# A hybrid two-layer trunk on one core: later constants, a mixing row in three transfers, and a shifted table of steps

## The reference, cut to what matters

```
h = rms_norm(x, norm_g[l]);  p = h @ w_in[l]                 # columns of p are split below
sb:  y_sb  = stick_breaking(sq, sk, sv) * silu(sg)           # 4 heads x 128
mla: q = rms_norm(rms_norm(c_q) @ mla_w_uq);  k, v from rms_norm(c_kv) @ mla_w_ukv and k_rope
     y_mla = block_causal_softmax(rope(q), rope(k), v) * silu(mg)      # 8 heads
rw:  rw_main += rw_mu[l] * (shift_by_one_token(rw_main) - rw_main)     # mixing row rw_mu
     kk = k * k_k;  kk = kk / |kk|                            # per head
     y_rw = group_norm(rwkv7_scan(r, decay, k, v, -kk, kk*a)) * silu(rg)
merged = sig(g_sb)*(y_sb @ w_br_sb) + sig(g_mla)*(y_mla @ w_br_mla) + sig(g_rw)*(y_rw @ w_br_rw)
x = x + merged @ w_out[l]
```

## Time and profile before

| | |
|---|---|
| median of three runs | 1680.75 us (1680.42 to 1682.27) |
| the profiled execution | 1682.79 us |
| its span | 1681.0 us |
| PE busy | 1665.9 us, 99% |
| DVE, ACT, POOL busy | 1154.5, 841.7, 489.8 us |
| granted TensorE clock | 1.00 throughout |

### The profile page before, as it was taken

The page is one execution under the profiler, slowest core; times in us unless marked ns, Lnnn a source line. Parts: engine busy times, 40 slices in busy tenths (PEclk is TensorE's granted clock), DMA queues, the critical chain, the costliest instruction groups (busy, mean ns, idle before and its releaser), DMA issues.

```text
span 1681.0 us, 21448 instructions
## 1 busy us (share of the span) xinstructions
PE 1665.9 (99%) x8010; PEld 1390.0 (83%) x8010; DVE 1154.5 (69%) x1667; ACT 841.7 (50%) x1221; POOL 489.8 (29%) x722
## 2 busy tenths in 40 slices
PE   7999999999999999999999999999999999999999
PEld 6878888888888888888888788888888888888887
DVE  4668775866976566886656786857778665578853
ACT  6544554435545455555454445534445544555542
POOL 1011313410343426362400112233103534245500
PEclk9999999999999999999999999999999999999999
DMA  8865656656665557785687656556566565668764
GB/s 260 262 179 184 185 166 189 183 159 189 180 183 172 176 163 235 234 307 188 207 264 229 180 175 178 187 163 200 162 180 181 168 177 177 187 211 289 262 193 158
DMA packets 176912, 332.72 MB, mean 198 GB/s; under 512 B 19516, under 2 KB 32746, under 8 KB 176808
## 3 DMA queue, kind: packets, MB, share of 16 engines
q1 hardware_dynamic: 167048, 297.86, 58.3%
q0 software_dynamic: 9584, 33.42, 5.7%
q10 hardware_dynamic: 176, 0.07, 0.0%
HBM read 311.14 MB, written 16.78 MB: 195 GB/s over the span
## 4 chain that ended last, share of the span: by engine, by line
PE 90%; DVE 4%; ACT 2%; DMA 1%; SPq 1%; issue 1%; POOL 1%; ACTq 0%; DVEq 0%
PE D L724 81%; PE B L724 8%; DMA ring<-in_w_in 1%; DVE w_lo L1416 1%; DVE arena L1416 1%; ACT w_hi L1043 1%; POOL arena L587 1%; ACT arena L1043 1%; DVE arena L1547 0%; PE B L915 0%; DVE xy L1416 0%; SPq L464 0%; ACT gev L1043 0%; PE B L894 0%; DVE ht_lo L1750 0%
## 5 line engine op out<-in xcount | busy, mean ns | idle before, releaser
L1416 DVE TENSOR_TENSOR w_lo<-ring,w_hi 128x1024 fp32r<-128x1024 f32 (+3 forms) x560 | 677.1, 1223 | 330.8 <-ACT w_hi L1043 321.9
L1043 ACT ACTIVATE w_hi<-ring 128x1024 fp32r<-128x1024 f32 (+3 forms) x560 | 575.0, 1038 | 486.1 <-PE D L724 379.4
L724 PE MATMUL D<-w_hi,ht_hi 128*128 128x512 f32 (+2 forms) x1728 | 680.7, 394 | 4.3 <-DVE w_lo L1416 4.1
L724 PE MATMUL D<-w_hi,ht_lo 128*128 128x512 f32 (+2 forms) x1728 | 665.5, 385 | 0.0
L724 PE MATMUL D<-w_lo,ht_hi 128*128 128x512 f32 (+2 forms) x1728 | 664.8, 385 | 0.0
L724 PEld LDWEIGHTS D<-w_hi,ht_hi 128*128 128x128 f32 x1728 | 325.0, 188 | 74.1 <-issue 8.8
L724 PEld LDWEIGHTS D<-w_hi,ht_lo 128*128 128x128 f32 x1728 | 324.6, 188 | 65.9
L724 PEld LDWEIGHTS D<-w_lo,ht_hi 128*128 128x128 f32 x1728 | 325.2, 188 | 58.9 <-issue 0.5
L626 POOL COPY arena<-arena 32x256 f32<-32x256 f32 x240 | 163.2, 680 | 144.6 <-DVE arena L1446 108.9
L724 PEld LDWEIGHTS B<-arena 128*128 128x128 f32 (+2 forms) x928 | 121.7, 190 | 20.8 <-issue 8.1
L1043 ACT ACTIVATE arena<-B 64x64 f32<-64x64 f32 (+6 forms) x186 | 54.9, 300 | 165.0 <-PE B L724 158.8
(11 more groups left out here) (163 smaller groups left out, 1386.8 us busy)
## 6 DMA issues: line engine op xcount, KB each, us to landing
ring<-in_w_in SPq DMA_DIRECT2D x368, 512.0 KB, 4.5
ring<-in_w_out SPq DMA_DIRECT2D x64, 512.0 KB, 5.2
ring<-in_w_br_mla SPq DMA_DIRECT2D x32, 512.0 KB, 5.5
gate_spill<-gev POOLq DMA_DIRECT2D x24, 512.0 KB, 4.7
arena<-gate_spill POOLq DMA_DIRECT2D x24, 512.0 KB, 5.7
ring<-in_mla_w_ukv SPq DMA_DIRECT2D x16, 512.0 KB, 4.4
ring<-in_w_br_rw SPq DMA_DIRECT2D x16, 512.0 KB, 5.2
ring<-in_w_br_sb SPq DMA_DIRECT2D x16, 512.0 KB, 5.4
```

Of the source, the lines that this page charges most:

```text
L724: return nc.tensor.matmul(o, a, b, start=start, stop=stop, skip_group_check=True)
L1043: return nc.scalar.activation(o, i, fn, **kw)
L1416: return v.tensor_tensor(o, a, b, op)
```

## The change

Six edits, as the diff shows: the constants are issued by POOL after the eviction of rk instead of before the shifts; the mixing row goes in three transfers of 512 columns ahead of the loads of chunks 11, 13 and 15; ACT's norm of kk stands one chunk later; the steps of the fourth pair get numbers of their own (`RW_LAST`), and those of the group norm and of one MLA entry are shortened, so that what comes after is nearly where it was; in `mla_prepare` on ACT the norm comes two beats after the second square instead of one, with one beat less behind it.

```diff
@@ -158,13 +158,14 @@
 AT_PAIRS = AT_DECAY + 5
 RW_STEPS = [1, 1.2, 1, 1.7, 2.96] + [0.92, 1.02] * LEVELS + [0.88] * 6
 LATENT_STEPS = [2, 2.5]
-GN_STEPS = [0.9] * 8
+GN_STEPS = [0.84] * 8
 ML_PREP, ML_VISITS = [1.1, 1.2, 1.3, 1.2, 1.4, 1.4], [2, 1.5, 1.4]
-ML_STEPS = ML_PREP + ML_PREP + ML_VISITS[:2] + [2.8] + ML_PREP + ML_VISITS[:2] + [3.4]
+ML_STEPS = ML_PREP + ML_PREP + ML_VISITS[:2] + [2.2] + ML_PREP + ML_VISITS[:2] + [3.4]
 ML_STEPS += ML_PREP + ML_VISITS + [0.8] * 6 + ML_VISITS
 SB_STEPS = [4, 3.5, 3]
 RW_BEATS, GN_BEATS, ML_BEATS, SB_BEATS = len(RW_STEPS), len(GN_STEPS), len(ML_STEPS), len(SB_STEPS)
-STEPS = RW_STEPS + LATENT_STEPS + 3 * RW_STEPS + GN_STEPS + ML_STEPS + SBH // 2 * SB_STEPS
+RW_LAST = [1, 1.2, 1, 1.7, 3.3] + [1, 1.1] * LEVELS + [0.88] * 6
+STEPS = RW_STEPS + LATENT_STEPS + 2 * RW_STEPS + RW_LAST + GN_STEPS + ML_STEPS + SBH // 2 * SB_STEPS
 AT_STEP = [sum(STEPS[:n]) for n in range(len(STEPS) + 1)]
 
 
@@ -480,8 +481,9 @@
                             sp.sem_inc(x_settled[l], 1)
                     if n == 2 * RING:
                         row(MU[:, 1536:1664], rw_mu[l, 1536:1664], mu_in[0][l])
-                    if n == 3 * RING - 1:
-                        row(MU[:, 0:1536], rw_mu[l, 0:1536], mu_in[1][l])
+                    for i in range(3):
+                        if n == 3 * RING - 1 + 2 * i:
+                            row(MU[:, i * 512:(i + 1) * 512], rw_mu[l, i * 512:(i + 1) * 512], mu_in[1][l])
                     if n == 3 * RING:
                         row(GR[:, 0:QK], mla_qn_g[l], rows_in[l])
                         row(GR[:, QK:2 * QK], mla_kn_g[l], rows_in[l])
@@ -541,11 +543,10 @@
 
                 pool.wait_ge(dense_ev[l], GI["wk"] + 1)
                 shift(PW, WK[:, :, 64:192], wk_shift[l])
-                if l == 0:
-                    pool.wait_ge(split_lo, END["wk"] + 2)
-                    pool.dma_start(con[:, P:K_END], consts[:, P:K_END]).then_inc(con_in, 16)
                 for i in range(3):
                     pool.wait_ge(dense_ev[l], GI["rr"] + i + 1)
+                    if l == 0 and i == 1:
+                        pool.dma_start(con[:, P:K_END], consts[:, P:K_END]).then_inc(con_in, 16)
                     shift(PV[:, :, i * 512:(i + 1) * 512], R[:, :, i * 512:(i + 1) * 512], r_shift[i][l])
 
                 pool.wait_ge(con_in, 16)
@@ -1203,11 +1204,11 @@
                 beat()
                 act.wait_ge(ml_ss, 8 * l + 2 * p + 1)
                 f(q2[:, :, :, 0:NOPE], MKV[:, b, :, :, 0:NOPE], ACT.Square).then_inc(ml_sq, 1)
-                beat()
+                beat(2)
                 act.wait_ge(ml_ss, 8 * l + 2 * p + 2)
                 link(f(qkss, qkss, ACT.Ln, scale=1.0 / QK, bias=eps))
                 f(qkss, qkss, ACT.Exp, scale=-0.5).then_inc(ml_rs, 1)
-                beat(4)
+                beat(3)
 
             def mla_pair(p):
                 act.wait_ge(ml_dve, 12 * l + 3 * p + 1)
@@ -1330,8 +1331,7 @@
                         last = f(t[:, h, :], B[2 * i + h][:], ACT.Sigmoid)
                 last.then_inc(lora_act[l], 1)
                 act.preload_act_table_set("natural_log_exp_and_others")
-                dense_to(AT_KK + 1)
-
+                dense_to(AT_KK + 2)
                 act.wait_ge(kk_ss, l + 1)
                 link(f(kss, kss, ACT.Ln, scale=2.0 ** 20))
                 f(kss, kss, ACT.Exp, scale=-0.5, bias=bias_kk).then_inc(kk_rs, 1)
@@ -1799,7 +1799,7 @@
                 tt(lat, lat, PW, ALU.add).then_inc(lora_dve[l], 1)
                 for i in range(3):
                     dense_to(AT_MIX[i])
-                    dve.wait_ge(mu_in[1][l], 16)
+                    dve.wait_ge(mu_in[1][l], 16 * (i + 1))
                     dve.wait_ge(r_shift[i][l], 16 * SHIFTS)
                     c = slice(i * 512, (i + 1) * 512)
                     link(tt(PV[:, :, c], PV[:, :, c], R[:, :, c], ALU.subtract))
```

## The result

| | before | changed |
|---|---|---|
| median | 1680.59 us (1679.96 to 1682.27, 6 runs) | 1687.21 us (1686.38 to 1688.82, 6 runs) |
| profiled execution | 1682.79 us | 1686.51 us |
| its span | 1681.0 us | 1684.8 us |

The ratio is 1.0038, with a 95% interval of 1.0027 to 1.0049: 4.5 to 8.2 us more. I forecast 1683.5, with 1680 to 1687 as range, and gave 0.59 to a difference too small to tell (under some 3.4 us) and 0.34 to slower. It is slower, and the median lies 0.2 us above the upper end of the range. The direction of the sum was right, its size was not: +2.7 forecast, +6.6 measured. The profiled executions differ by 3.7 only.

The account below looks back on a forecast made before the run. PE was taken as the bound (busy 1665.9 of 1681.0 us), so only its idle counted. −1.7 − 0.6 − 0.7 + 0 + 5.7 = +2.7 us on the median 1680.75 gave 1683.5, range 1680 to 1687.

Parts of the forecast that it names:

- The MLA norm: MLA preparation: pair 0's norm behind two more `w_hi` makes PE start chunk 147 2.8 us later per layer; together +5.7 us.
- No slack is left in that chain: MLA preparation: the delayed steps up to chunk 147's `w_lo` absorb nothing, so PE starts that chunk +2.8 us later.
- the clock falls: Rival: PE's 3.3 us idle at chunk 147 brings the lower clock, two chunks +5.5 us, median 1689; chance 0.03.
- The start of layer 1: Chunks 11 and 12: 512 KB less ahead of chunk 11's load removes PE's waits; −1.7 us, bounds −0.8 and −1.9.
- The constants: Ahead of rk's shift: shift at most 2.2 us late, covered by a lead of nearly three chunks; price 0.
- Layer 2's start: Start of layer 2: the mixing row's 0.44 us idle at 869.85 all goes; −0.6 us.
- The norm of kk: At 118.94: one more `w_hi` ahead of ACT's wait removes PE's 0.20 us wait in each layer; −0.7 us.
- The fourth pair: RWKV fourth pair: two old PE waits go (−1.0), new ones of 0.7 and 0.3 come; 0 us a layer.
- The rival that they multiply: Fourth pair: both old waits reappear one level later beside the new; +1.0 us a layer, median 1685.4; chance 0.17.
- The sum: Whole kernel: all terms together +2.7 us, giving a median of 1683.5.

Follow-up runs that it names:

- experiment 1: The changed kernel with the MLA preparation's norm moved back one beat, tables kept: 1682.23 us, ratio 1.0008 to the kernel before.
- experiment 4: The changed kernel with the group norm's steps 0.78 instead of 0.84, so later steps stand half a chunk earlier: 1681.26 us, ratio 0.9997 to before.
- experiment 2: The kernel before with only the MLA preparation's norm one beat later: 1682.26 us, ratio 1.0004 to before.
- experiment 3: The kernel before with only the step tables changed (fourth pair, group norm, one MLA entry): 1683.64 us, ratio 1.0015 to before.
- experiment 7: The kernel before with only the mixing row in three transfers: 1680.13 us against 1681.31, ratio 0.9992.
- experiment 6: The kernel before with only the constants issued eight chunks later: 1682.72 us, ratio 1.0004 to before.
- experiment 5: The changed kernel with the constants issued early again: 1686.66 us, ratio 1.0034 to the kernel before.

## Why the prediction was right or wrong, step by step

- **The MLA norm, +5.7.** Right in mechanism, and in size by some luck. The idle time at chunk 147 is 2.70 us in each layer, with surplus 2.86, against the 3.3 forecast, and the change against before with chunk 148 is +2.6 and +3.1, together 5.7. "No slack is left in that chain" was wrong by 0.45 us in layer 1: from L1462 to the `w_lo` of chunk 147 DVE took 5.64 us before (450.06 to 455.70) and 5.19 after (451.76 to 456.95). Chunk 148, late by 0.33, which the sum had only as a bound, made up for most of it. In layer 2 the forecast leant on a chunk 147 without a wait, which before has in one of its two profiles only. Experiments 1 and 4 take the loss away, experiments 2 and 3 show that neither half makes it alone. What stood beside it as a rival with 0.03 was part of the truth: *the clock falls*. I treated it as a case by itself, although it hangs on the very wait that I forecast. And I took its chance from the granted clock of 1.00 in the earlier trace rows, a window that begins some 17 us after the 5.7 us idle at the start. The matmuls right behind that idle time say something else. PE in the kernel before:

```profile
6.24 3.59 PE L797 MATMUL B<-con,xy 128*128 128x128 f32 x16
12.56 1.04 PE L797 MATMUL B<-con,xy 128*128 128x128 f32 x8
```

The sixteen behind the idle time start 0.21 us apart, the eight of the same shape later 0.11 apart, and all profiles have it so. The granted clock of the profile's rows reads 1.00 at both places, so that it is the lower level is not shown; but half the pace is what I should have seen, and it speaks for the rival. At chunk 147 the lower clock adds 1.6 to 2.8 us at every second of these waits or more, by the mean clocks of the lists one to two and a half microseconds in most executions: less than the 5.5 of the rival as I priced it.
- **The start of layer 1, −1.7.** The mechanism is borne out in part. With the row cut the wait at chunks 11 and 12 is gone in seven of eight profiles (experiment 4 has 0.26 at chunk 12), but with the row whole it is gone in two of six as well. Its size was taken from one execution; the runs of experiment 7 show −1.2, with an interval that takes in 0, and that includes layer 2's start. That the first profile after shows the whole −1.9 is luck as much as it is the edit. The three transfers' fixed cost showed nowhere. The 2.0 us that the prediction quotes for it from the Trainium skill, "DMA: Bandwidth & Descriptors", section "Anatomy of one DMA", is stated there for transfers that GpSimd issues; SP issues these.
- **The constants, 0.** Wrong, and this is the step of the sum that failed by most. I said that the lead of nearly three chunks covers them, with a shift at most 2.2 us late. The mixing came 3.8 us later in experiment 6, and the loads of the chunks were late with it (a load issued at 72.84 was used at 81.95). Trace: +0.7 alone, +1.3 and +1.6 in the two profiles of the changed kernel, but 0 and 0.5 in experiments 1 and 4. Why it differs so stays open: loads were as late there in experiment 5 without the constants.
- **Layer 2's start, −0.6.** Right by the two profiles compared, but by luck: four of the six profiles with the whole row have no such wait.
- **The norm of kk, −0.7.** Right by every trace; too small for the runs to tell.
- **The fourth pair, 0.** The two new waits came where I put them: the product behind gate8's eviction starts at 383.69, some 5.6 us after gate8, with a wait of 0.34 for the 0.7 forecast, and the one behind ukv0's eviction waits 0.35 for the 0.3. What I missed is that the removal at the first product is not whole; 0.36 stays behind it. So there are three slower starts of 0.36, 0.51 and 0.51 against two of 0.5, +0.4 a layer. The rival that they multiply decides from +0.35 on, as I wrote.
- **The sum.** +2.7 becomes +6 when the measured terms are put in: start −1.2 with layer 2, kk −0.7, constants +1.3, pair +0.8, MLA +5.7 is +5.9, and the clock brings it to 7 to 8, within the interval of 4.5 to 8.2. This adds terms from single profiles to terms from runs, so its agreement with the +6.6 shows the order of size and no more; against the forecast the constants, the clock and the pair are what was missing. The sum on the profile was made against an execution 2.2 us above the later median, and I did not ask which wait made it so.

## What to carry to other kernels

In a table of step positions two moves that cost little by themselves can meet: price each instruction at its place in the new order, with the `w_hi` or `w_lo` ahead of it that itself waits for the slowest engine. A wait of TensorE between bursts can have two prices, here its 2.7 us and up to 2.8 us of lower clock behind it; look for the second in more than one profile, and in the pace of the matmuls, not only in the clock of the rows. A wait on a transfer in a single profile is a sample: take two profiles of the kernel before, and compare their times with the median, before a gain is built on it. Bytes moved out of one busy stretch land in another; ask what stands behind them there, and how near the busiest engine will be by then.

## What the runs showed of the hardware

That the granted clock after the same idle time (2.69 to 2.71 us) was 0.50 three times and 1.00 three times, in experiment 5 in layer 1 and not in layer 2, I had not expected; and that the lower stretch ended after 8 to 14 matmuls with no change in the work. Two 512 KB loads issued behind 643 KB of constants and the shift took 9.1 and 8.8 us to land, against 4.7 and 4.9 in the kernel before. The constants are not all of that: in experiment 5, where they had been issued some 35 us earlier, the loads issued between 68.8 and 74.6 took 8.4 to 10.0 us.
